# A one-hot product for the first expert block, zero products ahead of the count, and a token end that starts with the decode rows

## What is computed

```python
h = rmsnorm(x, g_pre_ffn)                        # 520 tokens x 1024
logits = h @ w_router + b_router                 # 8 experts
probs = softmax(logits); top_p, top_i = top_k(probs, 2); top_p = top_p / sum(top_p)
y = 0
for e in range(8):
    y = y + gate[:, e] * ((silu(h @ wg[e]) * (h @ wu[e])) @ wd[e])   # 1024 -> 1408 -> 1024
x = x + rmsnorm(y, g_post_ffn)
```

## Time and profile before

| | |
|---|---|
| median of 3 runs | 1898.61 us (1898.02 to 1899.66) |
| profiled execution | 1896.83 us, of which the span of the trace is 1894.4 us |
| TensorE, busy share of the span | 89% |
| VectorE, ScalarE, GpSimd | 51%, 38%, 31% |
| mean granted TensorE clock | 0.938 of full |
| mean HBM traffic | 150 GB/s |

### The profile page before, as it was taken

How to read it: one execution, slowest core, us unless ns; L and a number is a source line. 1 busy time by engine, 2 the same in 40 slices (tenths; PEclk the granted TensorE clock), 3 DMA queues, 4 the chain that set the end, 5 groups by cost and what they waited for, 6 DMA issues and landing times.

```text
span 1894.4 us, 28758 instructions
## 1 busy us (share of the span) xinstructions
PE 1694.3 (89%) x11174; PEld 1528.2 (81%) x11174; DVE 965.1 (51%) x1127; ACT 727.7 (38%) x948; POOL 588.8 (31%) x332
## 2 busy tenths in 40 slices
PE   4898887899999997889899995699999999999991
PEld 4798667899999997889665593589898998989880
DVE  5897544311111004231684417467586775867755
ACT  4445443222222123122553313345454444544542
POOL 3333222255554342232000122242241423314232
PEclk8899898999999998999799997799999999999996
DMA  5424202144445232122534216669789697887924
GB/s 166 127 89 141 67 10 80 41 143 139 138 138 183 84 128 89 45 89 68 202 117 139 67 34 190 186 207 290 194 238 245 200 298 195 257 226 219 261 94 163
DMA packets 347699, 283.41 MB, mean 150 GB/s; under 512 B 11747, under 2 KB 311823, under 8 KB 347497
## 3 DMA queue, kind: packets, MB, share of 16 engines
q1 hardware_dynamic: 327845, 253.54, 46.1%
q10 hardware_dynamic: 16532, 16.57, 2.6%
q0 software_dynamic: 3264, 12.50, 1.7%
HBM read 248.19 MB, written 35.10 MB: 150 GB/s over the span
## 4 chain that ended last, share of the span: by engine, by line
PE 42%; issue 27%; POOL 12%; DVE 11%; ACT 4%; DMA 2%; SPq 2%; POOLq 0%; DVEq 0%; ACTq 0%
PE ps L2111 33%; POOL ea L837 9%; DVE cT L1476 3%; PE ps L2239 2%; POOL ea L839 1%; PE ps L2073 1%; DVE rstd L1323 1%; PE ps L2429 1%; PE ps L2136 1%; POOL wlo L724 1%; DVE zc L1791 1%; PE ps L2249 1%; DMA tmp<-in_conv_w 1%; PE ps L2063 1%; PE ps L2480 1%
## 5 line engine op out<-in xcount | busy, mean ns | idle before, releaser
L2602 PE MATMUL ps<-ejx,ewh 128*128 128x384 f32 x1408 | 405.3, 362 | 3.3 <-issue 1.9
L1970 DVE TENSOR_TENSOR ewl<-eraw,ewh 128x2048 fp32r<-128x2048 f32 (+1 forms) x144 | 303.9, 2112 | 185.7 <-ACT ewh L1254 185.4
L1254 ACT ACTIVATE ewh<-eraw 128x2048 fp32r<-128x2048 f32 (+1 forms) x144 | 255.2, 1773 | 311.2 <-PE ps L2605 168.4
L2111 PE MATMUL ps<-hh,whi 128*128 128x260 f32 x1504 | 315.7, 292 | 50.2 <-DVE hl L1706 27.5
L2605 PE MATMUL ps<-ejx,ewl 128*128 128x192 f32 x1408 | 353.9, 251 | 0.0
L837 POOL TENSOR_TENSOR ea<-eat,ea 128x128 fp32r<-128x128 f32 x88 | 181.7, 2065 | 433.6 <-ACT ea L1278 433.6
L2111 PE MATMUL ps<-hh,wlo 128*128 128x260 f32 x1504 | 308.4, 287 | 0.0
L2111 PE MATMUL ps<-hl,whi 128*128 128x260 f32 x1504 | 308.3, 287 | 0.0
L2111 PEld LDWEIGHTS ps<-hh,whi 128*128 128x128 f32 x1504 | 239.8, 194 | 55.4 <-issue 32.7
L730 POOL TENSOR_TENSOR wlo<-raw,whi 128x2048 fp32r<-128x2048 f32 x46 | 214.9, 4671 | 211.0 <-ACT whi L860 87.2
L2602 PEld LDWEIGHTS ps<-ejx,ewh 128*128 128x128 f32 x1408 | 265.9, 189 | 6.7 <-issue 6.7
(11 more groups left out here) (378 smaller groups left out, 2648.6 us busy)
## 6 DMA issues: line engine op xcount, KB each, us to landing
eraw<-in_w_gate_e SPq DMA_DIRECT2D x88, 512.0 KB, 4.8
eraw<-in_w_up_e SPq DMA_DIRECT2D x88, 512.0 KB, 6.2
eraw<-in_w_down_e SPq DMA_DIRECT2D x64, 512.0 KB, 5.7
eraw<-in_w_down_e SPq DMA_DIRECT2D x48, 256.0 KB, 2.7
xs<-zero ACTq DMA_DIRECT2D x10, 1152.0 KB, 4.8
raw<-in_w_gate_d SPq DMA_DIRECT2D x22, 512.0 KB, 4.0
raw<-in_w_up_d SPq DMA_DIRECT2D x22, 512.0 KB, 5.2
raw<-in_w_down_d SPq DMA_DIRECT2D x16, 512.0 KB, 4.3
```

The lines of the kernel that those rows point to most:

```text
L1254: e.activation(ewh[:, s, 0:n], eraw[:, u % RAW, 0:n], ACT.Copy).then_inc(ew_hi, 1)
L1970: e.tensor_tensor(ewl[:, s, 0:n], eraw[:, u % RAW, 0:n], ewh[:, s, 0:n].bitcast(F32), ALU.subtract)\
L2111: ins = e.matmul(ps[:, 2 * q + h, 0:HALF], w, xx[:, k, h * HALF:(h + 1) * HALF], start=opens, stop=closes)
L2602: e.matmul(ps[:, q, 0:2 * C], ewh[:, s, o:o + P], ejx[:, k, :, :].rearrange("p h n -> p (h n)"), start=(k == 0), stop=(k == KD - 1), skip_ ...
```

## The change

**Expert 0's first block.** VectorE takes of each token the lower of its two slot numbers (`own_slot`) and compares it with the columns 0 to 191: `oh[token, column]` holds the token's inverse root where they agree and 0 elsewhere. TensorE multiplies `xtk` with it, eight column groups by five token tiles, and so has the transposed, normed rows of block 0 in PSUM with neither scatter nor gather. The gain of the norm, which `htok` carries, is now applied by ScalarE and VectorE while they split (`first_rows_hi`, `first_rows_lo`), two narrow operations for each wide one. The load of `gtok` for block 0 is gone; the scatter stays for the other jobs. Since `ea` lies over `htok`, ScalarE waits for the scatter before it writes `ea` in job 0.

**Zero products and the count.** Three of the four zero products stand ahead of the wait for the mask, the fourth behind the one-hot products. The signal that frees the weight buffers (`ew_used`) is given right behind the count and no longer behind the job list.

**End.** The last result is copied out by ScalarE and VectorE together; the square root's table is loaded there; the decode tile goes first (`TAIL`); `gpost` lies in `tmp` and is loaded in job 0.

```diff
-        gpost = at("gpost", [P, D], F32, 86272)
+        gpost = tmp[:, :, :].rearrange("p a t -> p (a t)")[:, 0:D]
+        oh = at("oh", [P, NT + 1, C], F32, 0)
+        TAIL = [NT] + list(range(NT))
@@ sync
+            e.dma_start(gpost, row_broadcast(a["g_post_ffn"][1], [[1, D]])).then_inc(gp_in, 16)
             with e.Fori(1, nj) as j:
...
             e.sem_inc(ys_ready, 1)
-            e.dma_start(gpost[:, :], row_broadcast(a["g_post_ffn"][1], [[1, D]])).then_inc(gp_in, 16)
+            e.wait_ge(f_y, 1)
+            e.dma_start(y_sample.rearrange("b s d -> (b s) d"), fo[0:B, NT, :]).then_inc(y_out, 16)
             for i in range(NT):
-                e.wait_ge(f_y, i + 1)
+                e.wait_ge(f_y, i + 2)
                 e.dma_start(y_prompt[0, i * P:(i + 1) * P, :], fo[:, i, :]).then_inc(y_out, 16)
@@ gpsimd
+            e.iota(coli[:, :], pattern=[[1, C]], base=0, channel_multiplier=0).then_inc(io_ready, 1)
+            e.tensor_copy(colf[:, :], coli[:, :]).then_inc(io_ready, 1)
...
             e.wait_ge(xs_in, 160)
-            e.dma_start(gtok[:, 0, :], xs[C:C + P, :]).then_inc(g0_in, 16)
-            e.dma_start(gtok[0:CB, 1, :], xs[C + P:2 * C, :]).then_inc(g0_in, 16)
...
-            for i in range(NT + 1):
+            for i in TAIL:
@@ scalar
+            def first_rows_hi(c):
+                e.wait_ge(er_done, c + 1)
+                for k in range(2):
+                    kk = 2 * c + k
+                    ins = e.activation(ejx[:, kk, 0, :], ps[:, EB[eb_at(2 * KE + c)[0]], k * C:(k + 1) * C], ACT.Copy,
+                                       scale=gT[:, G_PRE_FFN + 8 + kk:G_PRE_FFN + 9 + kk])
+                ins.then_inc(ej_hi, 1)
...
+                    if first and u == 2:
+                        e.wait_ge(xs_in, 160)
...
+            e.wait_ge(ed_done, nj + 1)
+            e.wait_ge(ys_out, nj * 32 + 16)
+            for n in range(2):
+                e.activation(etok[0:CB, 1, 512 * n:512 * n + 512], ps[P - CB:P, 4 + n, :], ACT.Copy).then_inc(ey_low, 1)
+            e.activation(etok[:, 0, 512:1024], ps[:, 3, :], ACT.Copy).then_inc(ey_ready, 1)
+            e.preload_act_table(ACT.Sqrt)
@@ vector
             e.tensor_scalar(sloti[:, :, :], slf[:, :, :], float(C), None, ALU.add).then_inc(slots_ready, 1)
+            link(e.tensor_tensor(own_slot[:, :], slf[:, 0, :], slf[:, 1, :], ALU.min))
+            for i in range(NT + 1):
+                n = P if i < NT else B
+                e.tensor_scalar(oh[0:n, i, :], colf[0:n, :], own_slot[0:n, i:i + 1], rs[0:n, i:i + 1],
+                                ALU.is_equal, ALU.mult).then_inc(oh_ready, 1)
             row_out(1)
...
+            def first_rows_lo(c):
+                e.wait_ge(ej_hi, c + 1)
+                q = eb_at(2 * KE + c)[0]
+                for k in range(2):
+                    kk = 2 * c + k
+                    ins = e.scalar_tensor_tensor(out=ejx[:, kk, 1, :], in0=ps[:, EB[q], k * C:(k + 1) * C],
+                                                 scalar=gT[:, G_PRE_FFN + 8 + kk:G_PRE_FFN + 9 + kk],
+                                                 in1=ejx[:, kk, 0, :].bitcast(F32), op0=ALU.mult, op1=ALU.subtract)
+                ins.then_inc(eb_free[q], 1)
...
-            result_rows(nj + 1, nj * 32 + 16, nj * 2 + 2)
+            e.tensor_copy(etok[:, 0, 0:512], ps[:, 2, :]).then_inc(ey_ready, 1)
+            for n in range(2):
+                e.wait_ge(ey_low, nj * 2 + 1 + n)
+                e.tensor_tensor(etok[0:CB, 1, 512 * n:512 * n + 512], ps[0:CB, 4 + n, :],
+                                etok[0:CB, 1, 512 * n:512 * n + 512], ALU.add).then_inc(ey_ready, 1)
@@ tensor
+            def zero_rows(c):
+                for h in range(2):
+                    ins = e.matmul(ps[:, 2 + c, 256 * h:256 * h + 256], ones[:, :], zero[:, 0:256], start=True, stop=True)
+                return ins
+            for c in range(3):
+                zero_rows(c)
             e.wait_ge(mask_ready, 1)
...
-            for c in range(4):
-                if c == 3:
-                    e.wait_ge(slots_ready, 1)
-                for h in range(2):
-                    ins = e.matmul(ps[:, 2 + c, 256 * h:256 * h + 256], ones[:, :], zero[:, 0:256], start=True, stop=True)
-            ins.then_inc(ed_done, 1)
-            e.wait_ge(jobs_ready, 1)
...
             e.sem_inc(ew_used, len(DN_CUTS) - 1)
...
+            for c in range(4):
+                q = EB[eb_at(2 * KE + c)[0]]
+                for k in range(2):
+                    kk = 2 * c + k
+                    for i in range(NT + 1):
+                        n = P if i < NT else B
+                        if c == 0 and k == 0:
+                            e.wait_ge(oh_ready, i + 1)
+                        ins = e.matmul(ps[:, q, k * C:(k + 1) * C], xtk[0:n, i, kk * P:(kk + 1) * P], oh[0:n, i, :],
+                                       start=(i == 0), stop=(i == NT), skip_group_check=True)
+                ins.then_inc(er_done, 1)
+            zero_rows(3).then_inc(ed_done, 1)
+            e.wait_ge(jobs_ready, 1)
...
-            rows_in(g0_in, 32, None)
```

More of the change, by code:

```diff
@@ L273, in build @@
         gate = at("gate", [P, 2, NT + 1], F32, R + 3520)
+        oh = at("oh", [P, NT + 1, C], F32, 0)
+        coli = at("coli", [P, C], I32, R + 4736)
+        colf = at("colf", [P, C], F32, R + 5504)
+        own_slot = at("own_slot", [P, NT + 1], F32, R + 6272)
         frs = at("frs", [P, NT + 1, 2], F32, R + 3584)
@@ L339, in build @@
         gf_in = sem("gf_in")
-        rows_zero, xs_in, g0_in, gt_in = map(sem, "rows_zero xs_in g0_in gt_in".split())
+        rows_zero, xs_in, oh_ready, gt_in = map(sem, "rows_zero xs_in oh_ready gt_in".split())
         ew_in = [sem(f"ew_in{i}") for i in range(6)]
@@ L1261, in rows_hi, with expert_act @@
                              ACT.Copy).then_inc(ej_hi, 1)
-            def expert_act(j):
+            def first_rows_hi(c):
[5 more added lines that the diff above has]
+                ins.then_inc(ej_hi, 1)
+            def expert_act(j, first=False):
                 for u in range(PER_JOB):
@@ L1287, in _ @@
             for c in range(4):
-                rows_hi(c, c + 1)
-            expert_act(0)
+                first_rows_hi(c)
+            expert_act(0, True)
             with e.Fori(1, nj) as j:
@@ L1293, in _ @@
                 expert_act(j)
-            for i in range(NT + 2):
-                if i <= NT:
+            e.wait_ge(ed_done, nj + 1)
[4 more added lines that the diff above has]
+            e.preload_act_table(ACT.Sqrt)
+            for p in range(NT + 2):
+                if p <= NT:
+                    i = TAIL[p]
                     n = P if i < NT else B
@@ L1860, in _ @@
             inverse(5)
-            e.wait_ge(io_ready, 8)
+            e.wait_ge(io_ready, 10)
             e.wait_ge(small_in, 64)
@@ L2026, in _ @@
             for c in range(4):
-                rows_lo(c, c + 1)
+                first_rows_lo(c)
             expert_dve(0)
@@ L2576, in rows_in @@
                     q = EB[eb_at(2 * KE + c)[0]]
-                    if j is not None:
-                        eb_wait(j, 2 * KE + c)
+                    eb_wait(j, 2 * KE + c)
                     for k in range(2):
```

35 lines of the change are left out of this document (18 added, 17 removed).

## The result

| | before | after |
|---|---|---|
| median | 1898.61 us (5 runs, 1898.02 to 1901.97) | 1888.99 us (5 runs, 1878.46 to 1890.17) |
| profiled execution, span | 1896.83, 1894.4 us | 1885.58, 1883.6 us |
| mean granted TensorE clock | 0.938 | 0.943 |

What follows compares the result with a forecast made beforehand. TensorE is busy without a pause through the expert jobs, so only work outside could move much. An earlier, full-clock job 0 start (18.8 us) plus the end (2.1) gave 20.9: median 1877.7 us, range 1872 to 1886.

Steps and rivals of the forecast that it cites:

- Block, its length: TensorE's 80 one-hot records for expert 0: 15.4 us, 3.5 us of it at half clock; bounds 13.7 and 26.4.
- The range: Forecast span for the whole kernel's median: 1872 to 1886 us, around 1877.7, with 85 in 100 for the forecast.
- Rival (a): Clock stays at half through the whole one-hot block, 26.4 us; median 1892.7; 6 in 100.
- Rival (b): Weight loads in the one-hot block are not hidden: median 1888 at full clock, 1914 at half; 4 in 100.
- Rival (c): Job 0's early start outruns scatter or weight refills, losing up to all 16 us: about 1886; 5 in 100.
- The cover of 10 us: Job 0: refilled weight buffer there by 1199, wanted by ScalarE at 1208.6; scatter's wait likewise 10 us late enough.
- Fillers and count: Six zero products ahead of the mask's wait keep the count at full clock: gain 1.0 us, between 0 and 1.3.
- Behind the block: From the one-hot block's end at 1188.4 to the first expert matmul at 1190.4, between 1189 and 1193.5.
- the clock at job 0's start: Job 0's first 22 matmuls run at full clock, 3.0 us and not 5.9: gain 2.9 us.
- The end: After the last expert job: copies 1.9 us and decode tile first 1.4 gained, last store 1.2 lost; 2.1 us gain.
- The dips: Clock dips over transposes between expert jobs: two more or less are 3 us either way.

Runs made afterwards that it cites:

- e5: Changed kernel with the decode tile's one-hot product replaced by a second 128-row product of tile 3; block 15.85 us, median 1874.06 us.
- e7: Changed kernel with the decode tile padded with zeros to 128 rows, everything computed; block 15.39 us, median 1875.58 us.
- e14: The changed kernel with the decode tile padded to 128 rows, run again beside the changed kernel on one chip; block 15.46 us, median 1875.01 us.
- e10: Changed kernel with all 40 one-hot products only 8 rows high, so values are missing; block 25.93 us, median 1888.38 us.
- e13: Changed kernel with all 40 one-hot products 64 rows high, so values are missing; block 25.94 us, median 1889.13 us.
- e9: Changed kernel with the eight 8-row decode products ahead of the 32 of 128 rows, everything computed; block 18.3 us, median 1880.38 us.
- e2: Changed kernel with four more zero products (8 records) between the count and the one-hot block; block 16.37 us, median 1877.52 us.
- e8: Changed kernel with the decode tile padded to 128 rows and four more zero products between count and block; block 13.21 us, median 1880.01 us.
- e6: Changed kernel with all six filler zero products (12 records) behind the count and none ahead of the mask's wait; block 16.09 us, median 1875.52 us.

## Why the prediction was wrong

The working gave the profiled execution 1875.9 us; it took 1885.6, 9.7 more. The steps, each as forecast and as measured:

| step | forecast | measured | difference |
|---|---|---|---|
| start of the count | 1168.74 | 1170.57 | +1.8 |
| count's start to block's start | 4.3 | 4.0 | -0.2 |
| block | 15.4 | 26.7 | +11.3 |
| block's end to first expert matmul | 2.0 | 1.9 | -0.1 |
| first to last expert matmul (job 0 at full) | 643.7 | 642.2 | -1.4 |
| last matmul's end to end of the span | 39.1 | 37.7 | -1.4 |
| outside the span | 2.4 | 2.0 | -0.4 |

**Block, its length: this step failed.** It took the two prices of a record, and both held (0.32 measured for 0.33 at half clock, 0.163 for 0.171 at full). It then took from the zero products how long the half clock would last, 3.5 us, and carried that over to the block. The zero products are 128 rows high throughout. One product in five here is 8 rows high, and the step treated it as one more record: "8 column groups x 5 token tiles". With all products tall the block is 15.4 to 15.9 us (e5, e7, e14), and that it comes so near the forecast is in part luck: half clock lasted 4.4 to 5.3 us there and not 3.5, and the lower price made up for it. The trace of before held a sign of what was missed, in the attention, where 64-row products stand ahead of 128-row ones:

```profile
915.22 4.46 PE L2429 MATMUL ps<-qT,kT 64*128 64x512 f32 x8 [2.35 <-ACT wt L1162]
919.60 1.11 PE L2432 MATMUL ps<-future,eye 128*128 128x128 f32 x4
...
915.50:919.60 4.10, 4.10 (x8) 0.50 0.94 327
919.60:925.60 6.00, 6.00 (x25) 0.50 0.73 262
925.70:933.00 7.30, 7.30 (x37) 1.00 0.12 28
```

TensorE is busy there without a pause from 915.22 on, the clock is at half from 915.4, and it rises at 925.7, 10.5 us behind the first record and 6.1 behind the first of 128 rows. One such place proves nothing by itself, but it showed that 3.5 us need not hold for low products. Nor was 3.5 the only value for tall ones: job 0's matmuls, 128 rows high, ran at half for 5.9 us (1206.3 to 1212.2). The step's bounds, 13.7 and 26.4, were then its honest range, and 85 in 100 for a value near the lower end was too much.

**The range.** The first median, 1888.99 us, lies above 1886, but the changed kernel's later medians, 1885.1 and 1884.88, lie inside, as the profiled execution's 1885.6 does. That is luck and no support for the working: their blocks took 23.1 to 26.7 us where it had 15.4, and the end and the dips, each better than forecast, gave back some 3 us.

**Rival (a)** described what happened in the first result, with 6 in 100, for another reason than it gave: half clock through nearly all of the block (26.4 forecast, 26.7 measured). Its median of 1892.7 is too high by the end's additional gain and because the clock did rise for the last 4 us and job 0 began at full. In e10 and e13, where it is true throughout, the medians are 1888.4 and 1889.1. What it lacked was a reason to believe in it; the one that it named against itself, that the zero products raised the clock, holds for products of 128 rows.

**Rival (b)**, weight loads that are not hidden, is refuted: 80 records with changing weights of 128 rows in 13.2 to 15.9 us. The Trainium skill, page TensorE: Matmul & The Clock Gate, section The mechanism, lets a weight load overlap matmuls in flight only where its group of rows differs, though above that sentence it also lets one into a background weight buffer be pulled ahead. Here it is the other way about: where the rows stay the same nothing shows between records, and where they change from 128 to 64 or 8 it is 0.44 us.

**Rival (c)**, supply: TensorE waits on neither weights nor the scatter in job 0, in any of the versions, even with the first expert matmul 11 us sooner than in the changed kernel. The cover of 10 us held. The rival's price of about 1886 was not that of losing all 16 us, which comes to 1893.6 (1877.7 + 15.9).

**Fillers and count.** In the first result the count ran at full clock and VectorE's wait for it fell from 1.63 to 0.40 us, the forecast 1.0 us and a little more. But it was luck: in thirteen of sixteen executions with the fillers the clock had fallen by then. The single stretch of 4.7 us at full clock in the earlier trace rows was taken for a rule.

**Behind the block.** The 2.0 us held, and so did the clock at job 0's start, 2.9 us (1.00 in the last stretch of the clock above). The narrow operations took 0.73 a pair on each engine, where 0.64 was forecast.

**The end** gave 3.4 us and not 2.1. The copies gained 2.0 as forecast (1.9). From the first gather to VectorE's end it took 28.4 us (1852.20 to 1880.56) and not 29.2, since tile 0 was complete after 8.9 us and not 9.8: 2.3 gained for 1.4. The last store cost 0.8 for 1.2.

**The dips** came out 1.4 us in favour, inside the 3 us that were set: behind job 0's start the trace has four stretches at half clock and not five.

## What to carry to other kernels

Before counting a matmul as work that lifts TensorE's clock, look at its rows: in this kernel products of 8 and of 64 rows did not lift it in 25.8 us without a pause, and padding the 8-row tile with zeros to 128 rows, at the same 0.32 us per record at half clock and 0.163 at full, brought a block of 23 to 27 us to 15.4. A short tile in a loop of full ones costs twice, by the clock and by an idle time at each change, so pad it. Doing it apart took the block only to 18.3 us (e9), and where the clock is up already, a short tile costs only the changes of height (3.2 us here, e2 against e8). And when a step's two bounds are 13.7 and 26.4 us and the value between them rests on when the clock rises, the chance has to be spread over both ends.

## What the runs showed of the hardware

- **Height and the clock.** From half clock, f32 products with changing weights lifted it after 4.4 to 5.3 us when none was lower than 80 rows and at least four in five had 128, and never within 25.8 us when all had 64 or 8. The Trainium skill, page TensorE: Matmul & The Clock Gate, Part 1, has the clock go by how busy the array has been. In the traces of e10 and e13 the busy share was 1.00 over the whole block and the clock 0.50, so the busy share as a trace shows it does not tell the clock.
- **Falling is another matter than rising.** At full clock the same mix of 128 and 8 rows, gaps included, ran 16 us without a fall (e2, e6).
- **The change of height.** For these f32 products 0.44 us of idle time at half clock and 0.23 at full, which is 0.30 and 0.19 us more than a packed record takes, between 128 rows and 64 or 8, in both directions; none between 128 and 120 or 80. It stands in the rows of the weight loads as "issue"; the rows of the matmuls show TensorE as busy.
- **An idle time of 2.7 us** without work ahead of the count let the clock fall in thirteen of sixteen executions of the same instructions. An idle time of that length is neither safe nor surely harmful.
